# Taking the rotary rotations of two attention layers off TensorE, in a one-core kernel of three transformer blocks

## The reference, cut to what matters

```python
def apply_rope(x, cos, sin):
    x1, x2 = jnp.split(xf, 2, axis=-1)
    return concatenate([x1 * c - x2 * s, x2 * c + x1 * s])

# attention a: 8 heads of 64 over 2 key heads, all 64 columns are rotated
qa = apply_rope(qa_x.reshape(B, S, H_A, HD_A), cos_a, sin_a)
ka = apply_rope(ka_x.reshape(B, S, HKV_A, HD_A), cos_a, sin_a)
# attention b: queries of 8 heads of 64 + 32 from a latent of 384, keys and values from a latent of 256
q = (rms_norm_2(q_lat, g_qa) @ w_qb).reshape(B, T, H_B, NOPE_B + ROPE_B)
kv = (rms_norm_2(kv_lat, g_kva) @ w_kvb).reshape(B, T, H_B, NOPE_B + V_B)
qr_x = apply_rope(qr_x, cos_b, sin_b)      # the last 32 of a head's 96 columns
kr_x = apply_rope(krb_x[:, :, None, :], cos_b, sin_b)[:, :, 0]
```

## Time and profile before

| | |
|---|---|
| median of 3 runs | 2469.02 us (2467.23 to 2473.43) |
| the profiled execution: its own time | 2467.05 us |
| the profiled execution: its span | 2465.2 us |
| TensorE matmuls busy | 2370.0 us, 96% |
| VectorE busy | 1545.7 us, 63% |
| ScalarE busy | 1028.4 us, 42% |
| GpSimd busy | 533.7 us, 22% |
| granted TensorE clock, mean | 0.989 |
| DMA, mean | 81 GB/s |

### The profile page before, as it was taken

How to read it: one execution, slowest core, us unless ns; L and a number is a source line. 1 busy time by engine, 2 the same in 40 slices (tenths; PEclk the granted TensorE clock), 3 DMA queues, 4 the chain that set the end, 5 groups by cost and what they waited for, 6 DMA issues and landing times.

```text
span 2465.2 us, 37427 instructions
## 1 busy us (share of the span) xinstructions
PE 2370.0 (96%) x14791; PEld 1986.9 (81%) x14791; DVE 1545.7 (63%) x2602; ACT 1028.4 (42%) x1955; POOL 533.7 (22%) x380
## 2 busy tenths in 40 slices
PE   8988999999999999999999999999999999999998
PEld 6765767777788887679977899998876688889898
DVE  4757545553434336677467867975656786788774
ACT  3337542532222235563246433334435543654343
POOL 3005212320210212231014211023623200322021
PEclk9998999999999999999999999999999999999999
DMA  5231152354532311002300122223120024013332
GB/s 193 71 104 52 36 188 69 120 160 147 168 107 88 130 50 39 27 1 69 103 26 2 43 78 60 61 78 136 50 58 29 26 69 120 10 44 114 101 110 88
DMA packets 197168, 198.72 MB, mean 81 GB/s; under 512 B 15832, under 2 KB 189624, under 8 KB 196866
## 3 DMA queue, kind: packets, MB, share of 16 engines
q1 hardware_dynamic: 191106, 178.23, 23.4%
q10 hardware_dynamic: 5888, 18.09, 2.0%
HBM read 186.87 MB, written 9.44 MB: 80 GB/s over the span
## 4 chain that ended last, share of the span: by engine, by line
PE 83%; DVE 9%; ACT 4%; issue 3%; POOL 1%; SPq 0%; DMA 0%; ACTq 0%; DVEq 0%; POOLq 0%
PE PS L941 9%; PE PS L942 9%; PE PS L944 9%; PE PS L895 6%; PE PS L897 6%; PE PS L896 6%; PE PS L1063 5%; PE PS L1093 4%; PE PS L868 4%; PE PS L871 4%; PE PS L869 4%; PE PS L1077 3%; DVE WL L2447 1%; PE PS L1135 1%; DVE ST L2603 1%
## 5 line engine op out<-in xcount | busy, mean ns | idle before, releaser
L2447 DVE TENSOR_TENSOR WL<-WB,WH 128x2048 fp32r<-128x2048 f32 (+3 forms) x86 | 185.8, 2160 | 208.6 <-ACT WH L1692 199.2
L941 PE MATMUL PS<-HH,WH 128*128 128x512 f32 (+4 forms) x768 | 298.1, 388 | 4.4 <-DVE XTb L3019 1.5
L942 PE MATMUL PS<-HL,WH 128*128 128x512 f32 (+4 forms) x768 | 284.9, 377 | 0.0
L944 PE MATMUL PS<-HH,WL 128*128 128x512 f32 (+4 forms) x768 | 271.4, 377 | 0.0
L3576 POOL TENSOR_SCALAR SA<-SA,ST 128x768 f32<-128x768 f32 (+4 forms) x80 | 143.7, 1796 | 512.8 <-DVE ST L2615 512.8
L1708 ACT ACTIVATE WH<-WB 128x512 fp32r<-128x512 f32 x240 | 141.9, 624 | 148.5 <-DVE WB L2459 111.8
L1692 ACT ACTIVATE WH<-WB 128x2048 fp32r<-128x2048 f32 (+3 forms) x86 | 148.0, 1721 | 131.9 <-PE PS L944 67.4
L2472 DVE TENSOR_TENSOR WL<-WB,WH 128x512 fp32r<-128x512 f32 x240 | 182.6, 775 | 32.1 <-ACT WH L1708 32.0
L895 PE MATMUL PS<-SH,WH 128*128 128x384 f32 (+1 forms) x576 | 180.6, 314 | 1.2 <-DVE WB L2506 1.2
L941 PEld LDWEIGHTS PS<-HH,WH 128*128 128x128 f32 (+2 forms) x768 | 141.6, 184 | 48.4 <-issue 8.9
L897 PE MATMUL PS<-SH,WL 128*128 128x384 f32 (+1 forms) x576 | 180.0, 313 | 0.0
(11 more groups left out here) (461 smaller groups left out, 6056.3 us busy)
## 6 DMA issues: line engine op xcount, KB each, us to landing
WB<-in_w_in_dram SPq DMA_DIRECT2D x61, 1024.0 KB, 5.3
WB<-in_w_ff_dram SPq DMA_DIRECT2D x32, 1024.0 KB, 5.5
WB<-in_w_mod_dram SPq DMA_DIRECT2D x24, 1024.0 KB, 5.3
WB<-in_w_branch_dram SPq DMA_DIRECT2D x24, 512.0 KB, 3.4
WB<-in_w_o_dram SPq DMA_DIRECT2D x8, 1024.0 KB, 5.4
WB<-in_w_in_dram SPq DMA_DIRECT2D x14, 512.0 KB, 6.5
WB<-in_cmp_w_dram SPq DMA_DIRECT2D x4, 1024.0 KB, 5.6
WB<-in_w_mkv_dram SPq DMA_DIRECT2D x4, 1024.0 KB, 5.1
```

The source lines that it names most:

```text
L941: pe.matmul(D[0:m, d + o:d + o + w], h, xh[:, o:o + w], start=first, stop=False)
L942: pe.matmul(D[0:m, d + o:d + o + w], h, xl[:, o:o + w], start=False, stop=False)
L944: t = pe.matmul(D[0:m, d + o:d + o + w], lo, xh[:, o:o + w], start=False, stop=last)
L2447: dve.tensor_tensor(b.of(WL[i]), b.of(WB[b.n % NW]), b.of(WH[i]).bitcast(F32), ALU.subtract).then_inc(*done("wl", s))
```

## The change

Six things are changed.

1. A `wqb` block is copied into `WH` and `WL` with 128 columns per head in place of 96: the 96, and the two halves of the 32 rotary columns a second time in exchanged order (`Block.copies`). The query products then leave the turned half in the PSUM rows 96 to 127, and the eight `rotB` products of a layer's queries go. (The key's one stays.)
2. VectorE's part of the rotation in attention b is cut in two: `turned_sines` reads PSUM straight after the query product, for three of the heads ahead of the split of the next weights, and `add_cosines` comes later.
3. In attention a the five `rotA` products of a layer go. ScalarE makes the turned tile by four copies of 32 rows each, from PSUM to `RB` (`turned`).
4. The sine tables carry the sign.
5. The spreads are `transpose` in place of `matmul`, with the same operands.
6. The second value product of a half of attention b is issued behind the first two score units.

```diff
+    def copies(self, W, B):
+        if not self.turned:
+            return [(self.of(W), self.of(B))]
+        w = W[:, :, :].rearrange("p a b -> p (a b)")[:, 0:self.kt * 512].rearrange("p (a b) -> p a b", b=128)
+        b = self.of(B).rearrange("p k (h c) -> p (k h) c", c=96)
+        return [(w[:, :, 0:96], b), (w[:, :, 96:112], b[:, :, 80:96]), (w[:, :, 112:128], b[:, :, 64:80])]
...
@@ tensor_program @@
-                    t = pe.matmul(P("norm", N)[:, c * 128:(c + 1) * 128], RS[:, rs[N], c:c + 1].to_broadcast([128, 128]), cm("ident"),
-                                  start=True, stop=True)
+                    t = pe.transpose(P("norm", N)[:, c * 128:(c + 1) * 128], RS[:, rs[N], c:c + 1].to_broadcast([128, 128]), cm("ident"))
...
-                        D = slot(("qb", l, half, i), ("qbc", l, half, i))
+                        D = slot(("qb", l, half, i), ("qbc", l, half, i), ("rt", l, half, i))
-                            h, lo = wh[:, k, i * 96:(i + 1) * 96], wl[:, k, i * 96:(i + 1) * 96]
+                            h, lo = wh[:, k, i * 128:(i + 1) * 128], wl[:, k, i * 128:(i + 1) * 128]
...
-                        for i in (2 * p, 2 * p + 1):
-                            D = rope((half, i), ("rt", l, half, i))
-                            pe.wait_ge(*at("qbc", l, half, i))
-                            pe.matmul(D[0:96, 0:512], cm("rotB")[0:96, :], QB[0:96, i, 0:512], start=True, stop=True).then_inc(*done("rot", l, half, i))
...
-                    attend(att[f"b{l}{half}"])
+                    def last_values():
+                        yield
+                        values_of(1)
+                    values_of(0)
+                    attend(att[f"b{l}{half}"], last_values())
...
-                    D = rope(key, ("rt", l, *key))
-                    pe.wait_ge(*at(*(("qar", l, j - 1) if j else ("kar", l))))
-                    pe.matmul(D[:, 0:512], cm("rotA"), SA[sa[src]][:, 0:512], start=True, stop=True).then_inc(*done("rot", l, *key))
@@ scalar_program @@
-                act.activation(b.of(WH[homes[s][0]]), b.of(WB[b.n % NW]), ACT.Copy).then_inc(*done("wh", s))
+                for hi, w in b.copies(WH[homes[s][0]], WB[b.n % NW]):
+                    t = act.activation(hi, w, ACT.Copy)
+                t.then_inc(*done("wh", s))
...
+                def turned(j, scale):
+                    if j > 1:
+                        act.wait_ge(*at(*(("qra", l, j - 3) if j > 2 else ("kra", l))))
+                    for p in range(0, 128, 32):
+                        q = p + 32 if p % 64 == 0 else p - 32
+                        t = act.activation(RB[j % 2][p:p + 32, 0:512], P(f"kq{l}", j)[q:q + 32, 0:512], ACT.Copy, scale=scale)
+                    t.then_inc(*done("turned", l, j))
@@ vector_program @@
+                    def turned_sines(i):
+                        dve.wait_ge(*at("up", "q", *key))
+                        D = taken(("rope", *key), ("qr", *key))
+                        dve.tensor_tensor(D[64:96, 0:512], P("qb", *key)[96:128, 0:512], RPb[96:128, 1, :], ALU.mult).then_inc(*done("rt", *key))
...
                     begin(f"wqb{l}", half)
+                    for i in range(3):
+                        turned_sines(i)
                     begin(f"wkvb{l}", half)
                     if half:
                         los(phases[run[0]][0] + 4)
-                    for p in range(2):
-                        for i in (2 * p, 2 * p + 1):
-                            rope_b((half, i), QB[0:96, i, 0:512], ("qbc", l, half, i), ("qr", l, half, i))
+                    add_cosines(0)
+                    turned_sines(3)
+                    for i in range(1, 4):
+                        add_cosines(i)
```

More of the change, by code:

```diff
@@ L112 @@
     flat: bool = False
+    turned: bool = False
     ring: str = ""
@@ L1620, in tensor_program @@
                 ps.order = [0, 1, 2, 3]
-                for i, _ in enumerate(linear(f"kq{l}", hx(NT), lambda j: nt if 0 < j < 5 else NT,
-                                             lambda j: [("kar", l) if j == 0 else ("tokc", f"va{l}") if j == 5 else ("qar", l, j - 1)], pace=4)):
-                    if i % 2 and i > 1:
-                        turn_tile(i // 2 - 1)
+                drain(linear(f"kq{l}", hx(NT), lambda j: nt if 0 < j < 5 else NT,
+                             lambda j: [("tokc", f"va{l}") if j == 5 else ("turned", l, j)]))
                 attend(att[f"a{l}"], values())
@@ L1652, in tensor_program @@
             for j in range(8):
-                t = pe.matmul(D[:, j * 128:(j + 1) * 128], GM[:, 1, 1, j, 0:1].to_broadcast([128, 128]), cm("ident"), start=True, stop=True)
+                t = pe.transpose(D[:, j * 128:(j + 1) * 128], GM[:, 1, 1, j, 0:1].to_broadcast([128, 128]), cm("ident"))
             t.then_inc(*done("tr", "gp"))
@@ L2213, in scalar_program, with values_of @@
                                            ACT.Copy).then_inc(*done("kbc", l, half, i))
-                    for g in range(2):
+                    def values_of(g):
                         act.wait_ge(*at("up", "v", l, half, 2 * g + 1))
@@ L2327, in q_in @@
                     act.activation(D[:, 0:nt], P(f"kq{l}", j + 1)[:, 0:nt], ACT.Copy, scale=SC_A).then_inc(*done("qar", l, j))
+                    turned(j + 1, SC_A)
                 begin(f"kq{l}")
@@ L2331, in scalar_program @@
                 act.activation(KR[:, :], P(f"kq{l}", 0)[:, 0:NT], ACT.Copy).then_inc(*done("kar", l))
+                turned(0, 1.0)
                 q_in(0)
@@ L2446, in split_lo @@
                 i = homes[s][0]
-                dve.tensor_tensor(b.of(WL[i]), b.of(WB[b.n % NW]), b.of(WH[i]).bitcast(F32), ALU.subtract).then_inc(*done("wl", s))
+                for (lo, w), (hi, _) in zip(b.copies(WL[i], WB[b.n % NW]), b.copies(WH[i], WB[b.n % NW])):
+                    t = dve.tensor_tensor(lo, w, hi.bitcast(F32), ALU.subtract)
+                t.then_inc(*done("wl", s))
             def unit_sum(n):
```

56 lines of the change are left out of this document (36 added, 20 removed).

## The result

The changed kernel takes 2451.32 us in the median of 4 runs (2449.09 to 2452.71), the kernel before beside it 2469.51 (2467.23 to 2473.43): a ratio of 0.9934, interval 0.9919 to 0.9950. It is faster by 18.2 us by the medians (12 to 20 by the interval) and by 16.2 between the two profiled executions, where 28.8 were forecast, and lies just above the range. The profiled execution took 2450.88 us, its span 2449.1.

The account below looks back on a forecast made before the run. TensorE, 83% of the chain, was taken as the bound. Attention b 15.4, attention a 6.4 and spreads 7.0 made 28.8 us off 2467.05, 2438.2; plus 1.97 for the median, rounded to 2440, range 2430 to 2451.

Parts of the forecast that it names:

- All 4.5 us go: Attention a, layer 0: VectorE's 4.51 us wait for the last rotation vanishes; with one rotation (0.86), 5.4 us gained.
- counted from the second tile's end nothing is won, and only the one rotation before it remains: Attention a, layer 1: turned copies cost 3.0 us, a vanished wait returns 2.9; one rotation, 0.86, say 1.0 us, remains.
- Fewer rows hardly make one cheaper: Attention a: each 32x512 turned copy on ScalarE costs 0.50 us, 2.0 per tile, bounds 0.3 and 0.75.
- 9 x 0.65 = 5.9: Attention b: VectorE's nine rotary instructions left behind the split take 5.9 us, with the first maximum right behind them.
- TensorE [...] starts as before: Attention b, layer 1, first half: first key product waits for the first sine product until 1846.0, so TensorE's start is unchanged.
- worth what VectorE's queue lets through: Attention b: second value product, 2.2 us, fills TensorE's wait for the first exponential; its gain is within the 15.4 us.
- Spreads: Transposes in place of products: 64 spreads at 0.111 us each, taken as 7.0 us, bounds 4 and 8.
- the rival with the quarter: Spreads fall to a quarter: 3.6 us more gain plus what follows, 2436 us; chance 0.05.
- that of the repeated column: Spreads: transposes of a repeated column take two records like products, 7.0 and 1.3 us less gain, 2448.5; chance 0.06.
- TensorE's own sum: VectorE is not the limit at attention b's four starts: 37.3 us gained in all, 2431.7; chance 0.14.
- The clock: TensorE's clock falls at attention a of layer 1 or in the first block; two falls at 4 us, 2448; chance 0.12.
- The rival of dearer small pieces: Turned copies cost 0.75 us and the split's pieces twice their price: about 22.5 us gained, 2446.5; chance 0.12.

Follow-up runs that it names:

- e5: Changed kernel with one assignment added, giving the transposes of attention a's values the fourth PSUM tile, not the third; 2446.08 us, ratio 0.9914.
- e7: e2 with the transposes of attention a's values forced into the third PSUM tile; 2452.51 us, ratio 0.9945.
- e12: e6 with idle products on TensorE in the waits at the start of attention a; 2445.20 us, ratio 0.9910.
- e6: Changed kernel with all of attention a's projections one PSUM tile on, so the values' transposes get the fourth; 2444.52 us, ratio 0.9907.
- e8: e5 with one plain copy of 128x512 per tile in place of four turned ones, halves not exchanged; 2438.78 us, ratio 0.9886.
- e10: The kernel of e6 run once more, beside the changed kernel on one chip; 2445.04 us, ratio 0.9909.
- e4: Changed kernel with the second value product of each half of attention b back ahead of the scores; 2450.59 us, ratio 0.9934.
- e1: Kernel before with only the spreads changed, to transposes; 2459.77 us, ratio 0.9968.
- e3: Changed kernel with idle products on TensorE in the waits at the start of attention a; 2450.48 us, ratio 0.9931.
- e2: Changed kernel with attention a's rotations back on TensorE and no turned copies; 2445.98 us, ratio 0.9916.

## Why the prediction was wrong

**The step that failed** is in attention a, layer 0: "All 4.5 us go", and in layer 1 "counted from the second tile's end nothing is won, and only the one rotation before it remains". Both followed VectorE's queue up to the first maximum and stopped there. The queue has the order that they say: in the changed kernel the last low halves end at 1262.6 and the first maximum stands directly behind.

```profile
1258.67 3.91 DVE L3439 TENSOR_TENSOR QA<-SA,QA 64x768 fp32r<-64x768 f32 x4
1262.61 0.16 DVE L2623 COPY PS<-SK 128x1 f32<-128x1 f32 x1
1262.80 0.69 DVE L2625 TENSOR_REDUCE ST<-PS 128x1 f32<-128x513 f32 x1
```

What I left out is that the five rotations also took PSUM tiles by turns, and that removing them moves every later tile of that turn. The fourth score unit got a wait that belonged to the fifth. e5 and e7 show it from both sides: 2.7 and 3.3 us by the table when it is taken out, 2.3 and 2.6 when it is put in alone. These are 6.0 of the 9.0 us that attention a fell short; 1.3 more are the clock's (e12 over e6), and 1.7 remain. I had used this very rule at attention b, where I followed which tile the first key product takes, and not here.

**Attention a, what remains.** With the tile put right and the clock held (e12), layer 0 gains 4.7 where 5.4 were forecast, and layer 1 nothing where 1.0 was. The queues do what the forecast says, with a size off. "Fewer rows hardly make one cheaper" holds, but a turned tile's four copies take ScalarE 2.4 us, 0.60 each and not 0.50: the 0.50 was the distance behind a single copy, and the copies stand behind one another. In layer 1 the weights' split of the earlier trace rows is at 2074.04, which with the 20.6 us gained ahead is 3.1 later than before, where the forecast comes to 3.0 less 0.9. Two turned tiles on that path at 0.4 more each would be 0.8 of this 1.0, an estimate. That layer 0 hides all the copies isn't quite so: one copy per tile gains 0.9 to 1.5 us there (e8 against e12 and e5).

**Attention b**: 13.2 us by the table against 15.4, its spreads included. Three of its steps came as forecast: the sines ahead of the split, the split's pieces (0.5 us each on ScalarE and on VectorE, 1.04 in series at 942.15, forecast 1.0), and, in three of the four halves, the maximum directly behind the last cosine sum. The term that was mis-sized is "9 x 0.65 = 5.9": from 942.15 to 948.45 they take 6.3 us. 0.65 was the mean of the old order, which repeats sine, cosine and sum at steps of 0.62, 0.71 and 0.61 us. Now cosine and sum follow each other at 0.71 and 0.61 by turns, the steps around the one sine left among them are 0.79, 0.73 and 0.72, and the last sum is 0.71 ahead of the maximum: 0.70 each. All four halves have this 6.3, and four times 0.4 is 1.6 us of the 2.2 missing. In the first half of layer 1, where "TensorE [...] starts as before" was said, the first key product waits for the sine, as it was said to:

```profile
1832.26 0.47 PE L1579 MATMUL PS<-KVLh,WH 128*128 128x512 f32 x1 [2.47 <-DVE SD L3284]
```

With the 13.9 us that the table has ahead of the half, it starts within 0.1 us of where it did before (1846.10), so "as before" was right. But the clock falls behind this wait, and the first maximum then waits 0.25 us for scores, which the forecast named as a sign of being wrong. In e6 the wait is the same 2.47 us, the clock stays at 1.00, and the stage gains 7.4 and not 6.7; e10, the same kernel, has the fall again and 6.4. The value product behind the second score unit, "worth what VectorE's queue lets through", is worth 0.5 to 0.8 us in this half and nothing in the others (e4).

**Spreads**: 6.6 us outside attention b by the table of e1 against 7.0, half the records and 0.11 us each. The Trainium skill ("TensorE: Matmul & The Clock Gate", section "Terms") calls the mode 4x faster for FP32; the measured factor is 2, and the rival with the quarter is out, as is that of the repeated column.

**The rivals.** TensorE's own sum (2431.7) is out, since VectorE's nine instructions set the first maximum. The clock had the right signs, new falls at both starts of attention a, and nearly the right total, but for a wrong reason: holding the clock gives back 0.1 and 0.6 us (e3) and 0.5 to 1.4 (e12), not 4 each, and the loss is a wait that stands at full clock as well. The rival of dearer small pieces is half right: the turned copies cost 0.60 us and not the 0.75 that it takes, and the split's pieces what was forecast. None of the rivals was a tile, so the range, which was drawn from them, ended at 2451 by their sum and not by a bound for what wasn't looked at.

## What to carry to other kernels

Where buffers are given out by turns, removing an operation that took one moves every later user to another buffer, with another release in front of it: write down who gets which buffer before and after, and at which step the next stage first asks for it, before costing anything else. A clock that falls beside a new wait is a suspect only: fill the wait with idle work, and see whether time comes back. A turn of partitions in four copies cost four whole copies here. In layer 0, where ScalarE is idle between tiles, three of the four cost 0.9 us in all; in layer 1, where two engines pass work to and fro, 4.1.

## What the hardware showed unexpectedly

A fall of TensorE's clock isn't set by the code around it alone. e6 and e10 are one kernel, with the same wait of 2.47 us ahead of the first key product of layer 1's attention b: over 1820 to 1845 the granted clock is 1.00 in e6 and 0.93 in e10. In e1 attention a is word for word that of the kernel before, and starts 4.8 us earlier; the stretch from 1276 on has a clock of 1.00 before, and of 0.72 in e1:

```profile
1276.00:1282.00 6.00, 3.57 (x27) 2.92 (x26) 5.75 (x11) 2.42 (x6) 0.00 (x0) 1.00 0.00 0
```

```profile
1276.00:1282.00 6.00, 5.30 (x31) 4.74 (x31) 4.93 (x11) 4.15 (x9) 2.14 (x2) 0.72 0.01 3
```

The stage shows -0.5 in e1. In the table the stage between the layers, whose code is the same in all rows from e2 to e12, gains between -0.4 and 3.5 us, and -0.2 and 3.0 in e6 and e10. I take it that where the falls come relative to the work changes with the microsecond in which a stage begins; no run isolates that. It is as large as a term of a forecast. The first 900 us differ as much, 1.0 to 6.5 us, without any edit there, and the changed kernel run again shows 1.4 in place of 4.3. So differences under 2 us between medians say nothing here. What is said of less comes from single stages of one trace each, and those of layer 1's attentions differ by up to 1.0 us between e6 and e10.
